# Low parts of weights made by an accumulating DMA in place of VectorE, from the feed-forward block on

## The chip, the cores and the metric

One core of one Trainium2 chip runs the whole program. The metric is the device time of an execution in microseconds.

## What is computed

The reference is a transformer block followed by two retention layers, all in float32, for 512 tokens of width 1024 (528 with 16 meta tokens, padded for the attention). Cut to what matters here:

```
n = rms(h); z = n @ w_in                      # columns: q, k, v, glu, gates
h = h + (sigmoid(g_att)*attention + sigmoid(g_conv)*(conv_branch @ w_conv_out)) @ w_out
up = dwconv3(rms(h) @ w_up)                   # 1024 x 5632
h = h + (silu(gate) * val) @ w_down           # 2816 x 1024
x = rms(h)
for layer in range(2):
    proj = rms(x) @ w_in_2[layer]             # 1024 x 8192
    mix  = [gated short convolution, retention of 8 heads]
    x = x + rms(mix @ w_out_2[layer])         # 2048 x 1024
```

Nearly all of the work is products of activations with weights that are used once.

## The kernel before

TensorE multiplies in a float32r format that drops low bits. Each product is therefore made of three: every operand is split in a high part (the value rounded to float32r) and a low part (the value less the high part), and TensorE adds high x high, high x low and low x high into the same PSUM bank.

The weights come in *units* of 1024 rows by 256 columns (1 MB; smaller for the down projection), in an order fixed by `plan`. A unit is loaded by SyncE's queue into one of three raw tiles `raw0` to `raw2`, as runs of 256 floats; `load(u + 3)` waits for the low part of the last slot of unit u. A unit is cut into two *slots* of 8 blocks of 128x128: by column (`BY_COL`: all 8 row blocks, 128 of the 256 columns, so that a slot reads 8 runs of 512 bytes in each partition of the raw tile) or by k (`BY_K`: 4 row blocks, all 256 columns, 4 KB in one run). Down-projection slots have 3 row blocks, or 2 in the second group. Each slot has a place among three pairs of tiles `whi`, `wlo` (a fourth is used twice at the end of the first retention layer).

`split_hi(s)` is a ScalarE copy raw -> whi, `split_lo(s)` a VectorE subtraction raw - whi -> wlo. `split_hi(s)` waits for the load and for TensorE's last product of the slot that had the place before, `gone[before[s]]`. `take()` gives the next slot to the matmuls and lets `fill` emit the splits of the slots up to two ahead. `products` emits for each block and each part of the columns three matmuls; its first one waits for `t_w`, the token of the slot's low part.

Every engine has its own queue, a `Line`: instructions run in the order in which the Python program emits them, with semaphore waits between. ScalarE and VectorE run the splits and the work on the products' results in that one order. The order of work from the change on: the up projection in two groups of 24 and 20 slots (`tile`: one slot, 48 matmuls of 256 or 258 columns), each followed by the down projection of its part (`two_tiles`: 16 slots each); then for each retention layer four pairs of heads, each with 4 slots for query and key (by k, `two_tiles`), 4 for value and gate (by k) and 8 for the convolution branch (by column, kinds x, c, b, z), among whose matmuls the retention's small products stand as `pieces`; then the output projection in 16 slots (by k). GpSimd's queue `po` holds five instructions at the very start (memsets and an identity matrix) and nothing after.

Of the kernel before, what the change touches and what calls it, by code (L numbers as in the profile page):

```python
# [16 lines left out]
def flat(tokens):  # L17
    for t in tokens:
        if isinstance(t, list):
            yield from flat(t)  # L20
        elif t is not None:
            yield t


class Line:
# [7 lines left out]
        self.ops.append((list(flat(after)), emit, self.count.sem, 1 if mark else 0))  # L33
        return token

    def dma(self, after, dst, src, count):
        token = count.up(16)
        self.ops.append((list(flat(after)), lambda e: e.dma_start(dst, src), count.sem, 16))  # L38
        return token

    def play(self, eng):
# [11 lines left out]
def bass_diff_attention_block_then_retention_layers_kernel(  # L53
# [5 lines left out]
    F = mybir.dt.float32  # L59
    R = mybir.dt.float32r  # L60
    I32 = mybir.dt.int32
    ALU = mybir.AluOpType
    ACT = mybir.ActivationFunctionType
# [17 lines left out]
    with ctx:  # L81
# [103 lines left out]
        def sem(name):  # L185
            return ctx.enter_context(nc.semaphore(name))

        pe, dv, ac, po, sp = Line(sem("pe")), Line(sem("dve")), Line(sem("act")), Line(sem("pool")), Line(sem("sp"))
# [9 lines left out]
        def act(after, o, i, func, **kw):  # L198
            return ac.put(after, lambda e: e.activation(o, i, func, **kw))  # L199

        def tt(after, o, a, b, op):
            return dv.put(after, lambda e: e.tensor_tensor(o, a, b, op))  # L202
# [58 lines left out]
        plan = []  # L261

        def unit(src, slots):
            plan.append((src, slots))

        def cols(w, c0, r0=0, nk=KT, n=256):
            return w[128 * r0:128 * (r0 + nk), c0:c0 + n].rearrange("(k p) c -> p k c", p=128)
# [12 lines left out]
            unit(cols(w_conv_out[0], 256 * j), BY_COL)  # L280
        for j in range(4):
            unit(cols(w_out[0], 256 * j), BY_K)
        GROUPS = [(0, 6), (6, 11)]
        for a, b in GROUPS:
            for j in range(a, b):
# [35 lines left out]
        place = []  # L321
# [6 lines left out]
        def load(u, after):  # L328
            src = plan[u][0]
            n = src.shape[1] * src.shape[2]  # L330
            dst = RAW[u % 3][:, 0:n].rearrange("p (k c) -> p k c", k=src.shape[1])
            t = sp.dma(after, dst, src, raw_count[u % 3])
            loaded.append({k: t for k in range(src.shape[1])})
# [8 lines left out]
            loaded[u][half[0]] = t  # L342

        halves = []

        def split_hi(s):
            u, (k0, k1, c0, c1), _ = slots[s]
            src = plan[u][0]
            n = (k1 - k0) * (c1 - c0)
            raw = RAW[u % 3][:, 0:src.shape[1] * src.shape[2]].rearrange("p (k c) -> p k c", k=src.shape[1])  # L350
            raw = raw[:, k0:k1, c0:c1]
            hi = WHI[place[s]][:, 0:n].rearrange("p (k c) -> p k c", k=k1 - k0)
            lo = WLO[place[s]][:, 0:n].rearrange("p (k c) -> p k c", k=k1 - k0)
            used = extra_free if place[s] == 3 else []
            if before[s] is not None:
                used = [gone[before[s]]]
            halves.append((hi, lo, raw, act([loaded[u][k0], used], hi, raw, ACT.Copy)))

        def split_lo(s):
            u, _, last = slots[s]  # L360
            hi, lo, raw, t_hi = halves[s]
            t_lo = tt([t_hi], lo, raw, hi.bitcast(F), ALU.subtract)
            ready.append((hi, lo, t_lo))
            if last and u + 3 < len(plan):
                load(u + 3, [t_lo])

        def split(s):
            if len(halves) == s:
                split_hi(s)
            split_lo(s)  # L370
# [104 lines left out]
        def whole():  # L475
# [109 lines left out]
            def start():  # L585
# [7 lines left out]
                spread_tokens(0, d, 6)  # L593
                put_x([3], 0, 7, tk[3])
                split_lo(0)
                first_slot[0] = take(0)
                scale_x(0, 0)
# [12 lines left out]
                square_x(4)  # L610
                low_x(3, 0)
                split_lo(1)
                first_slot[1] = take(0)
                first_part(0, 0, 3)
# [774 lines left out]

            for g, (ja, jb) in enumerate(GROUPS):  # L1390
                atok = [None] * 12
# [647 lines left out]
```

How the kernel before makes its waits and increments, by code:

```python
    def play(self, eng):  # L41
        reached = {}
        for after, emit, sem, by in self.ops:
            for count, value in after:
                if reached.get(id(count), 0) < value:
                    eng.wait_ge(count.sem, value)
                    reached[id(count)] = value
            instruction = emit(eng)
            if by:
                instruction.then_inc(sem, by)
# [1933 lines left out]
        @block.sync  # L1984
        def _(eng):
            sp.play(eng)
            for count, value in finished:
                eng.wait_ge(count.sem, value)
```

## Time and profile before

| | us |
|---|---|
| median of 2 runs | 1889.04 (1887.94 to 1890.13) |
| span of the profiled execution, first to last instruction | 1885.5 |
| TensorE busy | 1867.1 (99%) |
| VectorE busy | 1130.1 (60%) |
| ScalarE busy | 737.5 (39%) |
| GpSimd busy | 1.2 |

The profiled execution is known by its span alone; the median of the runs is 3.5 us over it. In the profile PE is TensorE's matmuls and PEld its weight loads, DVE VectorE, ACT ScalarE, POOL GpSimd, SP SyncE; "L191" is a line of the kernel, here that of a helper, so that groups are told apart by their tiles: `wlo<-raw,whi` is an instruction that writes a low tile from a raw and a high tile. "x" is a number of instructions.

### The profile page before, as it was taken

Reading aid. Unit: us, or ns where it says so; the run is one execution under the profiler, and the core shown is the slowest. Engines: PE = TensorE matmul, PEld = TensorE weight load, DVE = VectorE, ACT = ScalarE, POOL = GpSimd, SP = SyncE. Lnnn points to the kernel's source line nnn. Section 1 sums busy time; section 2 is a strip of 40 time slices with the busy share of each in tenths; the row PEclk is TensorE's granted clock in tenths of the full one; section 3 lists DMA queues with packets and bytes.
Section 4 is the critical chain, followed back from the end, with each engine's and each line's share of the span. In section 5 each row is a group of like instructions: output and inputs, shape, how many; then the busy total and the mean of one; then the engine's idle time right before and its main releaser. Section 6 shows DMA issues by size and latency. Waiting matters only on the chain.

```text
span 1885.5 us, 28594 instructions
## 1 busy us (share of the span) xinstructions
PE 1867.1 (99%) x12262; PEld 1688.0 (90%) x12262; DVE 1130.1 (60%) x2035; ACT 737.5 (39%) x1379; POOL 1.2 (0%) x9
## 2 busy tenths in 40 slices
PE   8999999999999999999999999999999999999998
PEld 7999999877899988998898989898899898989887
DVE  5888897577657753666746363636266636454534
ACT  6222333677634432344433333333245333333322
POOL 0000000000000000000000000000000000000000
PEclk9999999999999999999999999999999999999999
DMA  5222222101222223223323233322333232223131
GB/s 185 94 90 90 71 94 87 64 24 46 68 73 92 95 89 107 90 78 94 107 83 102 78 90 90 89 90 80 100 90 90 73 96 78 90 71 108 68 123 45
DMA packets 151837, 163.64 MB, mean 87 GB/s; under 512 B 3495, under 2 KB 148192, under 8 KB 151711
## 3 DMA queue, kind: packets, MB, share of 16 engines
q1 hardware_dynamic: 151694, 161.82, 27.1%
q8 instruction: 96, 1.57, 0.3%
q14 instruction: 31, 0.25, 0.0%
q10 hardware_dynamic: 16, 0.00, 0.0%
HBM read 159.71 MB, written 2.10 MB: 86 GB/s over the span
## 4 chain that ended last, share of the span: by engine, by line
PE 98%; ACT 1%; DVE 1%; DMA 0%; issue 0%; SPq 0%; DVEq 0%
PE ps L191 95%; PE ps L196 2%; ACT nhi L199 0%; DMA xt<-in_x_dram 0%; ACT p L199 0%; DVE ast L973 0%; ACT L199 0%; DVE p L210 0%; DVE wlo L202 0%; ACT whi L199 0%; DVE m L202 0%; ACT ps L199 0%; DVE ga L210 0%; SPq L38 0%; ACT rbc L199 0%
## 5 line engine op out<-in xcount | busy, mean ns | idle before, releaser
L191 PE MATMUL ps<-nhi,whi 128*128 128x256 f32 (+3 forms) x2528 | 682.2, 319 | 3.6 <-DVE nlo L202 2.1
L191 PE MATMUL ps<-nhi,wlo 128*128 128x256 f32 (+3 forms) x2528 | 673.4, 316 | 0.0
L191 PE MATMUL ps<-nlo,whi 128*128 128x256 f32 (+2 forms) x2400 | 637.6, 318 | 0.0
L202 DVE TENSOR_TENSOR wlo<-raw,whi 128x1024 fp32r<-128x1024 f32 (+2 forms) x308 | 365.0, 1189 | 349.7 <-ACT whi L199 349.1
L191 PEld LDWEIGHTS ps<-nhi,whi 128*128 128x128 f32 x2528 | 426.2, 189 | 35.8 <-DVE nlo L202 2.3
L191 PEld LDWEIGHTS ps<-nhi,wlo 128*128 128x128 f32 x2528 | 425.5, 189 | 32.2
L191 PEld LDWEIGHTS ps<-nlo,whi 128*128 128x128 f32 x2400 | 400.8, 189 | 29.1
L199 ACT ACTIVATE whi<-raw 128x1024 fp32r<-128x1024 f32 (+2 forms) x308 | 314.6, 1026 | 261.4 <-PE ps L191 261.0
L210 DVE SCALAR_TENSOR_TENSOR c<-u,cv,c 128x514 f32<-128x514 f32 x240 | 163.2, 748 | 0.0
L191 PE MATMUL ps<-wlo,nhi 128*128 128x256 f32 x512 | 81.6, 281 | 0.0
L191 PE MATMUL ps<-whi,nhi 128*128 128x256 f32 x512 | 81.6, 281 | 0.0
L191 PE MATMUL ps<-whi,nlo 128*128 128x256 f32 x512 | 81.3, 281 | 0.0
L199 ACT ACTIVATE y<-zr,cf 128x512 f32<-128x512 f32 x44 | 35.8, 816 | 113.4 <-DVE zr L202 113.4
L191 PEld LDWEIGHTS ps<-whi,nhi 128*128 128x128 f32 x512 | 70.0, 189 | 0.6
L191 PEld LDWEIGHTS ps<-wlo,nhi 128*128 128x128 f32 x512 | 69.8, 189 | 0.0
L191 PEld LDWEIGHTS ps<-whi,nlo 128*128 128x128 f32 x512 | 69.6, 189 | 0.0
L191 PE MATMUL ps<-alo,whi 128*128 128x512 f32 x176 | 68.5, 389 | 0.0
L191 PE MATMUL ps<-ahi,whi 128*128 128x512 f32 x176 | 68.5, 389 | 0.0
L191 PE MATMUL ps<-ahi,wlo 128*128 128x512 f32 x176 | 68.5, 389 | 0.0
L210 DVE SCALAR_TENSOR_TENSOR y<-zr,cf,y 128x512 f32<-128x512 f32 x88 | 65.9, 748 | 1.8 <-ACT y L199 0.3
L207 DVE TENSOR_SCALAR nx<-ss 128x4 f32<-128x4 f32 (+2 forms) x26 | 4.3, 164 | 102.6 <-ACT ones_d L199 93.9
L199 ACT ACTIVATE ones_d<-ps,osc 128x128 f32<-128x128 f32 x64 | 23.5, 368 | 93.5 <-PE ps L191 91.9
(267 smaller groups left out, 2171.7 us busy)
## 6 DMA issues: line engine op xcount, KB each, us to landing
raw<-in_w_in_dram SPq DMA_DIRECT2D x90, 1024.0 KB, 5.5
raw<-in_w_up_dram SPq DMA_DIRECT2D x22, 1024.0 KB, 5.0
raw<-in_w_out_dram SPq DMA_DIRECT2D x20, 1024.0 KB, 5.1
raw<-in_w_down_dram SPq DMA_DIRECT2D x8, 768.0 KB, 4.9
raw<-in_w_down_dram SPq DMA_DIRECT2D x8, 640.0 KB, 4.6
raw<-in_w_conv_out_dram SPq DMA_DIRECT2D x4, 1024.0 KB, 5.2
xt<-in_x_dram SPq DMA_DIRECT2D x4, 512.0 KB, 5.5
raw<-in_w_in_dram SPq DMA_DIRECT2D x4, 512.0 KB, 8.2
```

The source lines that it names most:

```text
L191: return pe.put(after, lambda e: e.matmul(o, w, m, start=start, stop=stop_), mark)
L196: return pe.put(after, lambda e: e.transpose(o, i, idn), mark)
L199: return ac.put(after, lambda e: e.activation(o, i, func, **kw))
L202: return dv.put(after, lambda e: e.tensor_tensor(o, a, b, op))
L207: return dv.put(after, lambda e: e.tensor_scalar(o, a, s1, s2, op0, op1))
L210: return dv.put(after, lambda e: e.scalar_tensor_tensor(o, a, s, b, op0, op1))
```

## The change

For slots of units from the up projection on (`u >= up_units`), the low part is made in two steps: ScalarE writes the negated high part into the low tile, and then a DMA issued on GpSimd's queue adds the raw weights to it in place. The semaphore of that DMA, one for each of the four places, is what TensorE's first product of the slot and the next load into the raw tile wait for. Slots of earlier units stay as they were. The diff:

```diff
-    def dma(self, after, dst, src, count):
+    def dma(self, after, dst, src, count, **kw):
         token = count.up(16)
-        self.ops.append((list(flat(after)), lambda e: e.dma_start(dst, src), count.sem, 16))
+        self.ops.append((list(flat(after)), lambda e: e.dma_start(dst, src, **kw), count.sem, 16))
         return token
@@
         for j in range(4):
             unit(cols(w_out[0], 256 * j), BY_K)
+        up_units = len(plan)
         GROUPS = [(0, 6), (6, 11)]
@@
         halves = []
+        c_rest = [Count(sem(f"rest{i}")) for i in range(4)]
@@
             hi, lo, raw, t_hi = halves[s]
-            t_lo = tt([t_hi], lo, raw, hi.bitcast(F), ALU.subtract)
+            if u < up_units:
+                t_lo = tt([t_hi], lo, raw, hi.bitcast(F), ALU.subtract)
+            else:
+                t_neg = act([t_hi], lo, hi.bitcast(F), ACT.Copy, scale=-1.0)
+                t_lo = po.dma([t_neg], lo, raw, c_rest[place[s]], accum_op=ALU.add)
             ready.append((hi, lo, t_lo))
             if last and u + 3 < len(plan):
                 load(u + 3, [t_lo])
```

## Rows read from the trace of the kernel before

**Rows 1.** The page: busy time and share of the span; the chain's shares.
```profile
PE 1867.1 (99%) x12262; PEld 1688.0 (90%) x12262; DVE 1130.1 (60%) x2035; ACT 737.5 (39%) x1379; POOL 1.2 (0%) x9
...
PE 98%; ACT 1%; DVE 1%; DMA 0%; issue 0%; SPq 0%; DVEq 0%
```
**Rows 2.** Busy time by stretch: up projection, first layer, all from the change on.
```profile
core 0: us, PE busy (x) PEld busy (x) DVE busy (x) ACT busy (x) POOL busy (x), PEclk, DMA share, GB/s
539.51:679.35 139.84, 139.84 (x1174) 139.66 (x1173) 97.28 (x148) 60.35 (x79) 0.00 (x0) 1.00 0.25 83
913.48:1306.40 392.92, 392.92 (x2234) 341.87 (x2232) 206.58 (x403) 138.90 (x259) 0.00 (x0) 1.00 0.29 86
539.50:1885.50 1346.00, 1339.67 (x8118) 1194.06 (x8116) 724.10 (x1258) 489.82 (x812) 0.00 (x0) 1.00 0.28 88
```
**Rows 3.** Groups of instructions by shape, 539 us to the end: VectorE's and ScalarE's splits.
```profile
L202 DVE TENSOR_TENSOR wlo<-raw,whi 128x1024 fp32r<-128x1024 f32 x202 | 246.0, 1223 | 250.4 <-ACT whi L199 250.1
L202 DVE TENSOR_TENSOR wlo<-raw,whi 128x768 fp32r<-128x768 f32 x24 | 22.9, 958 | 43.3 <-ACT whi L199 43.3
L202 DVE TENSOR_TENSOR wlo<-raw,whi 128x512 fp32r<-128x512 f32 x8 | 5.5, 692 | 7.3 <-ACT whi L199 7.3
...
L199 ACT ACTIVATE whi<-raw 128x1024 fp32r<-128x1024 f32 x202 | 211.8, 1054 | 161.5 <-PE ps L191 161.2
L199 ACT ACTIVATE whi<-raw 128x768 fp32r<-128x768 f32 x24 | 20.1, 841 | 45.2 <-PE ps L191 45.2
L199 ACT ACTIVATE whi<-raw 128x512 fp32r<-128x512 f32 x8 | 5.0, 628 | 9.0 <-PE ps L191 9.0
```
**Rows 4.** Timeline of ScalarE in the up projection: start, duration, instruction, idle before.
```profile
603.39 1.04 ACT L199 ACTIVATE whi<-raw 128x1024 fp32r<-128x1024 f32 x1
...
608.92 1.04 ACT L199 ACTIVATE whi<-raw 128x1024 fp32r<-128x1024 f32 x1
611.86 0.82 ACT L199 ACTIVATE y<-zr,cf 128x512 f32<-128x512 f32 x1 [1.90 <-DVE zr L202]
612.58 1.04 ACT L199 ACTIVATE whi<-raw 128x1024 fp32r<-128x1024 f32 x1
...
618.61 1.05 ACT L199 ACTIVATE whi<-raw 128x1024 fp32r<-128x1024 f32 x1
```
**Rows 5.** Timeline of TensorE at the first products of two slots there.
```profile
610.72 0.40 PE L191 MATMUL ps<-nhi,whi 128*128 128x256 f32 x2
...
627.88 0.40 PE L191 MATMUL ps<-nhi,whi 128*128 128x256 f32 x2
```
**Rows 6.** Timeline of ScalarE in the first and the second down projection.
```profile
712.28 0.84 ACT L199 ACTIVATE whi<-raw 128x768 fp32r<-128x768 f32 x1 [3.29 <-PE ps L191]
...
720.44 0.84 ACT L199 ACTIVATE whi<-raw 128x768 fp32r<-128x768 f32 x1 [3.29 <-PE ps L191]
...
883.76 0.63 ACT L199 ACTIVATE whi<-raw 128x512 fp32r<-128x512 f32 x1 [2.04 <-PE ps L191]
...
890.56 0.63 ACT L199 ACTIVATE whi<-raw 128x512 fp32r<-128x512 f32 x1 [0.83 <-PE ps L191]
```
**Rows 7.** Timeline in the first retention layer: two high parts and their first products.
```profile
1019.90 1.04 ACT L199 ACTIVATE whi<-raw 128x1024 fp32r<-128x1024 f32 x1
...
1025.53 0.39 PE L191 MATMUL ps<-nhi,whi 128*128 128x512 f32 x1
...
1086.72 1.04 ACT L199 ACTIVATE whi<-raw 128x1024 fp32r<-128x1024 f32 x1
...
1092.97 0.48 PE L191 MATMUL ps<-nhi,whi 128*128 128x512 f32 x1
```
**Rows 8.** DMA issues: number, KB each, median us from issue to landing.
```profile
raw<-in_w_in_dram SPq DMA_DIRECT2D x90, 1024.0 KB, 5.5
raw<-in_w_up_dram SPq DMA_DIRECT2D x22, 1024.0 KB, 5.0
...
xt<-in_x_dram SPq DMA_DIRECT2D x4, 512.0 KB, 5.5
raw<-in_w_in_dram SPq DMA_DIRECT2D x4, 512.0 KB, 8.2
out_dram<-outs SPq DMA_DIRECT2D x3, 512.0 KB, 2.6
```
**Rows 9.** The loads' DMA queue: packets, MB, share of 16 engines over the span.
```profile
q1 hardware_dynamic: 151694, 161.82, 27.1%
```

## Prediction

> **What bounds the kernel now.** I read the page's busy shares and its chain first. TensorE is busy 1867.1 of 1885.5 us and owns 98% of the chain; VectorE stands at 60%, ScalarE at 39%, GpSimd at nothing [rows 1]. The table of stretches comes next, for the part that the change touches, 539.5 us to the end: TensorE is busy 1339.67 of 1346.00 us at full granted clock, VectorE 724 us, ScalarE 490 us, GpSimd 0, and the DMA engines 28% [rows 2]. So at most 1346.0 - 1339.7 = 6.3 us can be gained, 0.3%, whatever VectorE is relieved of. A faster result by over 2% (38 us, about what a measurement of this kernel can tell from no change) is out of reach. The question is only whether TensorE starts to wait.
>
> It waits when a slot of weights is not ready. Each slot has 3 buffers in turn; the high part of slot s+3 may be written once slot s is used up, and its products begin two slots later. What must fit between is the budget of the new operation.
>
> **The change, part by part.** From the feed-forward block on there are 236 slots: 204 of 1024 elements a partition, 24 of 768, 8 of 512 (two of the 1024 had their high part before the window, hence 202 in the rows) [rows 3].
>
> Removed: 236 subtractions on VectorE, 246.0 + 22.9 + 5.5 = 274 us with two slots short, and before each the wait for ScalarE behind which all later VectorE work stood [rows 3]. Off the path: worth nothing beyond the 6.3 us.
>
> Added on ScalarE: 236 negating copies. Their nearest row is the high part itself, 1054 ns for 1024 elements and 841 ns for 768 [rows 3]. 204 x 1.05 + 24 x 0.84 + 8 x 0.63 = 240 us, which takes ScalarE from 490 to 730 of 1346 us. ScalarE mostly waits for others behind a high part, so this hides as load; in the chain of one slot it counts in full, in place of the 1.22 us subtraction, and I charge it to the budget below.
>
> Added on GpSimd: 236 accumulating DMAs from SBUF to SBUF, each waiting for its negated copy. Nothing else is queued there, so the wait holds back only the next DMA. TensorE now waits for the landing. The SP queue waits for it too: the load of unit u+3 is behind it, and behind that load only the following loads. A load lands 5.0 us after its issue [rows 8], and the raw tile is wanted some four slots (over 20 us) later, so up to about 15 us of lateness is free there.
>
> **The budgets.** From the start of a high part to its first product, less the high part and the negated copy (2 x 1.04 us for 1024 elements):
> - Feed-forward, up: high parts at 603.39, 608.92, 612.58 and 618.61 us [rows 4]; a slot is 48 matmuls, and counting them from the product at 610.72 [rows 5] a slot lasts 5.72 us, so the four first products are at 610.72, 616.4, 622.2 and 627.88 [rows 5]. Leads 7.3, 7.5, 9.6, 9.3; budgets 5.2, 5.4, 7.5, 7.2, mean 6.3. The pattern repeats over 44 slots. The short ones come from ScalarE's order: the high part stands behind tile work that waits for VectorE.
> - Down: two slots last 8.16 us in the first group (712.28 to 720.44) and 6.80 in the second (883.76 to 890.56) [rows 6]; less two copies of 0.84 that is 6.5 and 5.1 us.
> - Retention layers: ScalarE's order leaves most slots 7 to 11 us, but in every pair of heads three are tight: the second and third of the query/key products (the second counted to 4.2 us in the same way; the third from 1019.90 to 1025.53 [rows 7], 5.6 - 2.1 = 3.5 us), and one among the convolution slots (1086.72 to 1092.97 [rows 7]: 6.25 - 2.08 = 4.2 us); the first convolution slot has 7.4. There are 8 pairs of heads in two layers.
>
> **The unknown, L, from negated copy to landing.** No row has an accumulating DMA, one from SBUF to SBUF, or one from GpSimd. From below: 512 KB stored in 2.6 us [rows 8]. That fits every budget. From above: the slowest 512 KB load took 8.2 us, and a second stream to be read as in a 1 MB load adds up to 5.0 [rows 8]: 13.2 us. Between: slots cut by k are runs of 3 to 4 KB; the 512 KB load with such runs took 5.5 us [rows 8], and the extra read stream and GpSimd's work I put at 0.5 us net, since SBUF is nearer than HBM: L = 6 us, and 5.4 for the smaller down slots. Slots cut by column (44 - 2 in up, 64 in the layers) take 512-byte runs of the raw tile, 1024 of them, and read the copy as well. The 1 MB loads move 1024 packets in 5.0 to 5.5 us [rows 8]; a packet holds an engine 27.1% x 1885.5 x 16 / 151694 = 54 ns [rows 9], so 64 more per engine for the second stream add 3.5 us: L = 9 us. I take 6 and 9, as these rows are the nearest in run and count of packets; 2.6 and 13.2 stay for the range.
>
> **The sum.** Where all slots are short, the loop goes round once in three slots, so an overrun costs a third per slot. Where one is short between long ones, it is paid in full, once.
> - Up: (9 - 6.3) / 3 x 44 = 40 us.
> - Down: nothing in the first group, 0.3 / 3 x 16 = 2 in the second, and 3 for the late high parts at the entries: 5 us.
> - Query/key: 6 - 3.5 = 2.5, one delay for both tight slots, 8 times, less in the first pair of the second layer, which is split otherwise: 18 us.
> - Convolution slots: (9 - 4.2) + (9 - 7.4) = 6.4, 8 times: 51 us.
> - Output projections (32 slots, all by k, budgets mostly 7 to 8.5): 5 us for their entries.
>
> Together 119 us: 1885.5 + 119 = 2004.5. The runs shown have a median 3.5 us over that span, so 2008 us.
>
> The Trainium skill prices the same DMA otherwise. "DMA: Bandwidth & Descriptors", section "Anatomy of one DMA — SWDGE (gpsimd) path", gives a GpSimd-issued DMA about 2.0 us plus its bytes over 436 GB/s. An estimate from that page is 3.2 us for 512 KB, and the sum above would be about nothing. For 1 MB it would say 4.4 us where the loads here took 5.0, from another queue [rows 8]; no run here shows it for an accumulation. The same page, under "Why small descriptors are slow (HBM only)", says that SBUF to SBUF copies don't suffer from short runs.
>
> **Rivals.**
> 1. *Hidden* (the other side: not slower). L stays under about 5 us for both kinds of slot, as the 2.6 us store suggests. It decides at the shortest budgets, 3.5 to 5.2 us. Then only scattered tenths are lost and up to 6.3 gained: 1883 to 1910, middle 1892 us. For it: SBUF on both sides, DMA engines 72% idle. Against: a load of the same size took 5.5. This is what the first rule of the Trainium skill would give.
> 2. *Run length doesn't count*: L = 6 everywhere. Up: the overruns 0.8 and 0.6 in two of four slots, at most 9 us; convolution slots 6 - 4.2 = 1.8, 8 times, 14; the rest as in the sum, 28. 1889 + 51 = 1940 us. It is the case in which the second rule of the Trainium skill holds.
> 3. *Rate, not latency.* If a packet costs 54 ns whatever its size and both streams are fetched as 1024 packets, a slot by column holds each engine 2 x 64 x 54 ns = 6.9 us, and its share of a load 32 x 54 ns = 1.7. 8.6 us exceeds the slot's 5.7: 106 x 2.9 = 307 us, plus 28 elsewhere: 2224 us. It decides where the accumulation takes over 4.0 us of every engine, or GpSimd over 5.7 us to describe 1024 runs. For it: every packet is short; against: the packets measured came from HBM. The same end is reached by a cast from float32 to float32r done element by element.
> 4. *Gain*: the freed VectorE lets ScalarE start high parts earlier and L is short; 6.3 us at most, 1883 us. It can't pass 2%.
>
> **Chances.** Forecast (long runs 6, short 9, give or take 2) 0.37; hidden 0.25; run length without weight 0.13; rate 0.22; gain 0.03. The predicted time is the likeliest case, 2008 us, whose own range is 1955 to 2090 us. The upper bound L = 13.2 (8.2 for long runs) gives 101 + 13 + 38 + 118 + 10 = 280, or 2169 us. The range must take in the hidden case and half of the rate case: 1886 to 2200 us. Slower by over 2% is the forecast, the rate case and most of the second rival, 0.69; within 2% 0.29; faster 0.02.
>
> **What would show it.** Rows of the changed kernel: high part, negated copy and the TensorE row that waits for a DMA into the low tile. Right: landings 6 and 9 us after issue, TensorE's idle time falling on "DMA wlo", about a third of it in the up stage, almost none in the first down group; VectorE down by 274 us and ScalarE up by 240. A wait of ScalarE's tile work behind the copies, or of SP's loads so long that ScalarE waits for raw, would be a step I costed at nothing. The prediction is wrong if the landings are short (TensorE still busy 99%), or if the DMA share nears 1 or GpSimd's issues follow each other without a pause (rate).

## The result and the profile after

The changed kernel takes 2037.72 us (2033.94 to 2041.51, 2 runs) against 1889.04: 1.0787 times the time before, 95% interval 1.0697 to 1.0877. The prediction was 2008 us, in a range of 1886 to 2200. The profiled execution has a span of 2032.0 us, 146.5 more than before; the medians are 148.7 apart. Further down, a time given without an interval is one execution. The two executions of the changed kernel are 7.6 us apart, so a difference of that size between single executions says nothing.

The page after: busy time, the chain's shares by engine and by line, the two DMA queues, and the issues from number and KB to median us to landing. They answer to [rows 1, 8, 9].

```profile
PE 1917.3 (94%) x12262; PEld 1716.6 (84%) x12262; DVE 865.2 (43%) x1799; ACT 977.7 (48%) x1615; POOL 277.8 (14%) x245
...
q0 software_dynamic: 128960, 118.50, 41.0%
q1 hardware_dynamic: 151694, 161.82, 25.9%
...
PE 70%; DMA 14%; ACT 8%; DVE 5%; issue 2%; POOL 0%; SPq 0%; DVEq 0%; ACTq 0%; POOLq 0%
PE ps L191 69%; DMA wlo<-raw 14%; ACT wlo L199 2%; ACT whi L199 2%; PE ps L196 2%; ACT ones_d L199 1%; DVE y L210 1%; DVE sz L210 1%; DVE zr L202 0%; DVE pa L202 0%; ACT xa L199 0%; ACT nhi L199 0%; DVE na L202 0%; ACT sw L199 0%; DVE na L210 0%
...
wlo<-raw POOLq DMA_DIRECT2D x204, 512.0 KB, 6.5
...
raw<-in_w_up_dram SPq DMA_DIRECT2D x22, 1024.0 KB, 6.5
...
wlo<-raw POOLq DMA_DIRECT2D x24, 384.0 KB, 5.0
```

TensorE has the same 12262 matmuls but is idle for 2032.0 - 1917.3 = 114.7 us, 96 more than before, and the chain now holds 14% of DMA and, ahead of it, the two ScalarE copies. It is also *busy* for 50 us more, with the same work. The table of stretches (columns as in [rows 2]) shows the main reason: the granted clock is under full, 0.97 from the change on, where before it was 1.00. Matmul by matmul, 35 of the 50 us lie in stretches at the lower level of the clock, 11 in the matmuls next to a wait, and 4 elsewhere.

```profile
539.51:701.60 162.09, 147.33 (x1190) 145.63 (x1188) 71.11 (x124) 84.65 (x103) 35.01 (x23) 0.97 0.92 154
...
965.90:1389.50 423.60, 402.64 (x2234) 346.63 (x2232) 134.27 (x341) 207.86 (x324) 76.89 (x64) 0.98 0.84 161
539.51:2032.00 1492.49, 1389.35 (x8134) 1223.48 (x8132) 462.17 (x1024) 728.07 (x1046) 274.70 (x234) 0.97 0.82 159
```

The waits of TensorE from the change on (us in total, times, longest) name their cause:

```profile
PE ps L191 <- DMA wlo<-raw: 85.7, 45, 5.3
...
PE ps L191 <- DVE y L210: 6.7, 4, 2.2
...
PE ps L191 <- DVE qr L202: 2.5, 1, 2.5
```

One slot of the up projection in the timeline (ScalarE, GpSimd and TensorE; other rows of the stretch are left out):

```profile
640.55 1.04 ACT L199 ACTIVATE whi<-raw 128x1024 fp32r<-128x1024 f32 x1
641.63 1.06 ACT L199 ACTIVATE wlo<-whi 128x1024 fp32r<-128x1024 f32 x1
...
642.98 1.55 POOL L38 DMA_DIRECT2D wlo<-raw  x1 [6.11 <-ACT wlo L199]
...
651.45 0.77 PE L191 MATMUL ps<-nhi,whi 128*128 128x256 f32 x2 [3.41 <-DMA wlo<-raw]
...
652.87 0.63 PE L191 MATMUL ps<-nhi,whi 128*128 128x256 f32 x2
```

High part and copy take 2.1 us, as priced. The DMA is issued 0.3 us after the copy's end and lands 8.3 us after its issue (a load of 1 MB is under way for most of that time), and TensorE has stood for 3.41 us. Its matmul pairs then take 0.63 to 0.77 us in place of the 0.40 of [rows 5], for a while.

Counting the matmuls of each stage gives the length of the stages in both traces:

| stage | before | after | more | predicted | TensorE's waits, more |
|---|---|---|---|---|---|
| ahead of the change | 539.3 | 541.8 | 2.5 | 0 | -0.4 |
| up projection | 254.2 | 291.8 | 37.6 | 40 | 27.4 |
| down projection | 119.7 | 132.4 | 12.7 | 5 | 7.6 |
| query, key | 181.9 | 209.0 | 27.1 | 18 | 21.9 |
| value, gate | 184.6 | 186.5 | 1.9 | 0 | 3.4 |
| convolution slots | 422.6 | 466.9 | 44.3 | 51 | 22.2 |
| output projections | 180.4 | 200.8 | 20.4 | 5 | 14.3 |
| sum (2.8 us of output follow) | 1882.7 | 2029.2 | 146.5 | 119 | 96.4 |

The last column is the idle time before the stage's own matmuls; it is what the prediction's sum forecast. In the columns ahead of it a stage runs from its first matmul to the next stage's first, so the wait for a stage's first slot stands in the row of the stage before: 7.4 us of waits for other stages' first slots stand in the row of the convolution slots. What the sum of "more" has beyond the sum of waits is slower matmuls.

### The profile page after: what moved, and what is told of

The parts are those of the page before. It is cut to its first block, busy times and chain, and to the rows that moved or that the text cites. A ratio compares the mean times of both kernels' runs of the same rounds, so it can differ in the third digit from the quotient of the medians.

```text
span 2032.0 us, 28897 instructions
## 1 busy us (share of the span) xinstructions
PE 1917.3 (94%) x12262; PEld 1716.6 (84%) x12262; DVE 865.2 (43%) x1799; ACT 977.7 (48%) x1615; POOL 277.8 (14%) x245
## 3 DMA queue, kind: packets, MB, share of 16 engines
q0 software_dynamic: 128960, 118.50, 41.0%
## 4 chain that ended last, share of the span: by engine, by line
PE 70%; DMA 14%; ACT 8%; DVE 5%; issue 2%; POOL 0%; SPq 0%; DVEq 0%; ACTq 0%; POOLq 0%
PE ps L191 69%; DMA wlo<-raw 14%; ACT wlo L199 2%; ACT whi L199 2%; PE ps L196 2%; ACT ones_d L199 1%; DVE y L210 1%; DVE sz L210 1%; DVE zr L202 0%; DVE pa L202 0%; ACT xa L199 0%; ACT nhi L199 0%; DVE na L202 0%; ACT sw L199 0%; DVE na L210 0%
## 5 line engine op out<-in xcount | busy, mean ns | idle before, releaser
L191 PE MATMUL ps<-nhi,whi 128*128 128x256 f32 (+3 forms) x2528 | 694.1, 324 | 75.1 <-DMA wlo<-raw 62.5
L191 PE MATMUL ps<-nhi,wlo 128*128 128x256 f32 (+3 forms) x2528 | 683.2, 320 | 0.0
L191 PE MATMUL ps<-nlo,whi 128*128 128x256 f32 (+2 forms) x2400 | 647.6, 322 | 0.0
L38 POOL DMA_DIRECT2D wlo<-raw x236 | 276.6, 1172 | 1728.1 <-ACT wlo L199 1707.7
L191 PEld LDWEIGHTS ps<-nhi,wlo 128*128 128x128 f32 x2528 | 433.6, 193 | 33.2
L191 PEld LDWEIGHTS ps<-nlo,whi 128*128 128x128 f32 x2400 | 409.0, 193 | 30.1
L199 ACT ACTIVATE wlo<-whi 128x1024 fp32r<-128x1024 f32 (+1 forms) x236 | 241.6, 1024 | 7.4
L202 DVE TENSOR_TENSOR wlo<-raw,whi 128x1024 fp32r<-128x1024 f32 x72 | 88.1, 1224 | 48.0 <-ACT whi L199 47.8
L202 DVE TENSOR_TENSOR zr<-ps,rbc 128x514 f32<-128x514 f32 x44 | 30.4, 694 | 180.0 <-PE ps L191 175.0
L202 DVE TENSOR_TENSOR sd<-ps,far 128x512 f32<-128x512 f32 x16 | 11.0, 687 | 167.3 <-PE ps L191 167.3
```

Of the source, the lines that this page charges most:

```text
L191: return pe.put(after, lambda e: e.matmul(o, w, m, start=start, stop=stop_), mark)
```

## The experiments

Three theories stand against each other. A: TensorE waits for landings that come later than the slot's budget; what makes a landing late (run length, second read stream, loads beside it, GpSimd) is open within it. B: the copies, 240 us of them, disturb ScalarE's order. C: the DMA engines, with a share of 0.82 to 0.92, set the pace.

**The addition on VectorE.** Copies as in the change, no DMA:

```diff
-                t_lo = po.dma([t_neg], lo, raw, c_rest[place[s]], accum_op=ALU.add)
+                t_lo = tt([t_neg], lo, raw, lo.bitcast(F), ALU.add)
```

> The negated copies stay on ScalarE, the addition of the raw weights is done by VectorE in place of the DMA. Theory A (TensorE waits for the landing of the DMA, 6.5 us after its issue, and for nothing else of the change): the loss is gone, 1889 us within 5. Theory B (the 240 us of copies on ScalarE delay the tile work and with it TensorE): most of the loss stays, over 1960 us. Theory C (the DMA engines, busy 80 to 96%, set the pace): 1889 as well, but then with the load's landings back from 6.0-6.5 to 5.0-5.5 us.

Measured: 1908.39 us, 1.0105 times before (1.0088 to 1.0122). So the DMA bears some 129 of the 149 us. B is right in a smaller way: the copies cost 20 us, which the prediction had not priced. Its trace places it:

```profile
PEld ps L191 <- DVE wlo L202: 15.4, 12, 2.6
...
PE ps L191 <- DVE wlo L202: 11.6, 12, 2.1
```

TensorE waits 12 times for a low part that is a copy later than before, mostly where slots follow each other closely: the stages down (7.7 us) and query/key (5.6).

**Slots by k alone, slots by column alone.**

```diff
-            if u < up_units:
+            if u < up_units or slots[s][1][3] - slots[s][1][2] == 128:
```

and in the other kernel `> 128`.

> Only the slots cut by k are made by the DMA, those cut by column by VectorE as before. Theory A: the up projection and the convolution slots lose nothing, the down, query/key and output stages keep their loss (13 + 27 + 20 us in the changed kernel), less where it came from the collision with a neighbour cut by column: 1889 + 50, 1930 to 1950 us. Theory C (rate): with 0.5 MB every second slot only the engines are half free and nearly all loss goes: under 1905.

> The complement: only slots cut by column (half of the up stage and the convolution slots, 106 of 236) by the DMA. Theory A: the up and convolution stages keep their losses (38 + 44 us), the others lose at most what a landing into their first slot costs: 1965 to 1985 us. The losses of this run and of the one with slots by k add up to the whole, 147 us, within 20. Theory C: they add up to less than half of it.

Measured: 1972.58 us with slots by k alone, 1958.09 with slots by column alone. Over the 1888.62 us of the kernel before, measured beside them, that is 84.0 and 69.5 us, together 153.5 against the 149 of the full change: the losses add up, so the bulk is not a shared rate (C), which would vanish when half of the DMAs are gone. But both runs missed their ranges, since the split between the two kinds was wrong: slots by k cost 84, not 50 (1930 to 1950 us were expected), and slots by column 69.5 (1965 to 1985 us were expected). With slots by k alone the down stages lose 19.7 us, query/key 36.1, outputs 23.6, and the convolution slots 0. TensorE's waits for slots by k are not much longer than in the full change, 52.9 against 47.2 us, and in the query/key stages they are no longer, 20.7 against 21.9. What is longer is the time at the lower level of the clock, 27.3 against 13.7 us in the query/key stages. Another part of the miss is in the counting: the expected 50 us were worked out from the rows of the down, query/key and output stages, and waits for their first slots stand in the rows ahead of them.

**One run in place of eight.** For slots by column the DMA reads one run of 4 KB; the kernel leaves out that the right weights are added.

```diff
+                if slots[s][1][3] - slots[s][1][2] == 128:
+                    n = hi.shape[1] * hi.shape[2]
+                    raw, lo_ = RAW[u % 3][:, 0:n], WLO[place[s]][:, 0:n]
...
+                t_lo = po.dma([t_neg], lo_, raw, c_rest[place[s]], accum_op=ALU.add)
```

> Leaves out that the right weights are added: for slots cut by column the DMA reads the first 1024 elements of the raw tile in one run of 4 KB a partition instead of 8 runs of 512 bytes; bytes, waits and counts of DMAs are the same. If run length counts (theory A): landings for them fall from 7.2-8.0 us after issue to the 4.5-5.5 of the slots cut by k, GpSimd's instruction from 1.55 to 0.86 us, and 82 us of loss in the up and convolution stages fall to about 20: 1955 to 1980 us. If it does not count: 2030 to 2040 us.

Measured: 1987.42 us, so 50 of the 149 us go when the runs are long; 1955 to 1980 were expected. The page's queue row and issue row:

```profile
q0 software_dynamic: 33984, 118.50, 32.2%
...
wlo<-raw POOLq DMA_DIRECT2D x204, 512.0 KB, 5.6
```

The same 118.5 MB go in 33984 packets in place of 128960, the median landing comes 0.9 us earlier and GpSimd's instruction takes 0.86 us in place of 1.55:

```profile
603.93 0.86 POOL L38 DMA_DIRECT2D wlo<-raw  x1 [6.49 <-ACT wlo L199]
```

The up and convolution stages lose 34 us in place of 82, where 20 were expected.

**Small loads.** The kernel leaves out seven eighths of each weight load, so most products use old weights.

```diff
+            if u >= up_units + 3:
+                t = sp.dma(after, dst[:, 0:1, :], src[:, 0:1, :], raw_count[u % 3])
...
```

> Leaves out seven eighths of each weight load from the fourth unit of the feed-forward block on (one row block of eight is loaded, so most products use old weights); every wait, split and accumulating DMA is unchanged. Theory A1 (a landing has a floor of 6.4 us for slots cut by column and 4.5 by k after its issue, and 1 to 5 us more come from the load that shares the engines): landings stay at the floor, and the loss falls from 147 to 50-80 us: 1940 to 1970 us. Theory A2 (loads do not matter, late landings have another cause such as GpSimd's queue): landings of 8 to 12 us remain and the time is 2025 to 2040 us. Theory C (the DMA engines' rate sets the pace): without 7/8 of the loads the loss vanishes, under 1900.

Measured: 1986.41 us, 98.5 over the 1887.9 before. Without seven eighths of the loads 51 us less are lost; two thirds remain with the landings alone:

```profile
q0 software_dynamic: 128960, 118.50, 42.4%
q1 hardware_dynamic: 59918, 64.69, 10.1%
...
wlo<-raw POOLq DMA_DIRECT2D x204, 512.0 KB, 6.4
```

From the end of the copy a slot by column lands after 6.7 us at best and a full one by k after 4.8, here as in the full change; there the means over all slots were 7.5 and 8.4 us (up, convolution), 6.8 (query/key), 6.0 (value/gate) and 5.4 (down), with single ones up to 13.0, where here they are 7.0, 7.2, 5.1, 5.1 and 4.4, up to 9.0. The floor costs more than the expected 50 to 80 us, so the run missed its range; C is out as a cause of these two thirds, for it called for under 1900.

**The negation on VectorE.**

```diff
-                t_neg = act([t_hi], lo, hi.bitcast(F), ACT.Copy, scale=-1.0)
+                t_neg = ts([t_hi], lo, hi.bitcast(F), -1.0, ALU.mult)
```

> The negated copy is made by VectorE (tensor_scalar by -1) in place of ScalarE, the DMA is unchanged. Theory A (a chain of high part, copy, DMA against a budget): each chain is shorter by what the copy saves and the 1 us delay of ScalarE's own order is gone, which cost 20 us in the run with the addition on VectorE: 2005 to 2025 us. Against it: VectorE then waits for the high part again, as before the change; if that order is what sets the late high parts, the time stays at 2030 to 2045.

Measured: 2029.71 us, 8 less than the change, no more than the changed kernel's two executions are apart. It is at the edge of the second of the two outcomes: which engine negates matters little beside the landing.

**A plain copy, from two queues.** Both kernels leave out the addition.

```diff
-                t_lo = po.dma([t_neg], lo, raw, c_rest[place[s]], accum_op=ALU.add)
+                t_lo = po.dma([t_neg], lo, raw, c_rest[place[s]])
```

and in the second kernel `sp.dma([t_neg], lo.bitcast(F), raw, c_rest[place[s]])`.

> Leaves out the addition: the same DMA on GpSimd's queue only copies the raw weights over the negated high part. If the second read stream of the accumulation takes engine time (as the prediction charged, 3.5 us for short runs): landings 1.5 to 3 us earlier, the DMA queue's share down from 41% to under 30%, time 1960 to 1990 us. If the accumulation is free: landings, share and 2038 us unchanged within 8 us.

> The same plain copy (addition left out), issued on SyncE's queue, where the loads are, instead of GpSimd's. If GpSimd's making of descriptors is a part of the latency: landings 1 us earlier than in the plain copy on GpSimd's queue, and 10 to 25 us less in time. Against it: SyncE waits for each landing before it issues the next load, so the copies of the next slot queue behind that wait; if this dominates, high parts come to wait for raw and the time is longer than the plain copy's by over 10 us.

Measured: 1931.71 us on GpSimd's queue, faster than the 1960 to 1990 expected, and 1932.18 on SyncE's, neither of the two outcomes expected. The rows of the first and then of the second:

```profile
q0 software_dynamic: 128960, 118.50, 26.8%
...
wlo<-raw POOLq DMA_DIRECT2D x204, 512.0 KB, 3.8
...
wlo<-raw POOLq DMA_DIRECT2D x24, 384.0 KB, 3.7
```

```profile
wlo<-raw SPq DMA_DIRECT2D x204, 512.0 KB, 3.5
...
wlo<-raw SPq DMA_DIRECT2D x24, 384.0 KB, 4.4
```

Adding in place of copying is the largest single price: the same packets take 41.0% of 2032 us against 26.8% of 1930 (103 and 64 ns a packet), the median landing is 2.7 us later, and the time 106 us longer. For a copy, the queue that issues matters little: the landing is 0.3 us later at the median from GpSimd (3.8 against 3.5 us), and the time is the same. No run issues an accumulation from another queue.

The prices of these runs (20, 50, 51 and 106 us) overlap and do not add up to the 149: each says what goes away when one ingredient is taken out of a landing that is late by all of them.

**The low parts last.** The matmuls of a slot in another order, so that the DMA is wanted two thirds of a slot later; the same in the kernel before as a control.

```diff
-            for n, k in enumerate(ks):
-                for c, parts in enumerate(dst):
-                    wh, wl = hi[:, base + n, 128 * c:128 * c + 128], lo[:, base + n, 128 * c:128 * c + 128]
-                    for i, (w, m) in enumerate(((wh, xh), (wh, xl), (wl, xh))):
+            for i, (lw, m) in enumerate(((0, xh), (0, xl), (1, xh))):
+                for n, k in enumerate(ks):
+                    for c, parts in enumerate(dst):
+                        w = (lo if lw else hi)[:, base + n, 128 * c:128 * c + 128]
...
-                            if n == 0 and c == 0 and i == 0 and j == 0:
-                                wait.append(t_w)
+                            if n == 0 and c == 0 and j == 0 and i != 1:
+                                wait.append(t_lo if i else t_hi)
...
```

The loops of the value/gate stages and of the last output projection are changed in the same way.

> The changed kernel with the three products of a slot in another order: all high x high, then all low(activation) x high, then all high x low parts of the weights; the first matmul of a slot waits for the high part alone and the first of its last third for the DMA. Same matmuls, same DMAs. Theory A (landing against budget): every budget grows by two thirds of a slot, 3.8 us (2.7 in the down stages), to 7.3 and more, over most landings (5 to 8 us after the copy); the loss of 147 us falls to 0 to 20: 1889 to 1910 us, the clock back at full and the DMA engines busier than before (over 0.9). Theory C (rate of the DMA engines): the order of products changes nothing, over 2000 us.

> The control: the same order of products in the kernel before, with VectorE's low parts. 1889 us within 5, as TensorE is busy throughout already. If it is slower or faster by more, the order itself has a price or a gain that must be taken out of the run with the DMA.

Measured: 1912.37 us with the DMA, 1.0124 times before (1.0109 to 1.0139), 2 us above the range expected, and 1883.20 us for the control, 0.9974 times before (0.9964 to 0.9984), 5 us faster than before and 1 us outside its range. 125 of the 149 us are gone with every DMA in place, of which the order by itself gives 5, while the landings are no earlier (7.2 us) and the engines busier:

```profile
PE 1871.6 (98%) x12262; PEld 1688.4 (88%) x12262; DVE 865.2 (45%) x1799; ACT 976.8 (51%) x1615; POOL 277.7 (15%) x245
...
q0 software_dynamic: 128960, 118.50, 43.8%
...
wlo<-raw POOLq DMA_DIRECT2D x204, 512.0 KB, 7.2
```

```profile
744.00:860.00 116.00, 114.18 (x958) 113.58 (x957) 49.41 (x73) 65.35 (x77) 29.95 (x20) 1.00 1.07 180
541.00:1900.00 1359.00, 1337.10 (x8066) 1188.73 (x8065) 451.86 (x1001) 722.68 (x1034) 274.62 (x234) 0.99 0.90 173
```

This settles A against C: at a DMA share of 0.90 over the whole rest of the kernel TensorE is busy for 98% of it, and in the second group of the up projection at a share of 1.07 as well. The share is a sum of packet times and can pass 1, so packets of the two queues overlap, and a share near 1 doesn't mean that the engines have no more to give. What remains against the control, 29 us, lies for the most part at the passage between the two retention layers (8.8 us in the first output projection and 8.7 in the query/key stages behind it, with waits of 6.08 and 4.71 us), in the up projection (5.8) and in the last projection (5.3, with a wait of 3.68). The control is a quarter of a per cent faster than the kernel before; it is the best version found, and it has no accumulating DMA.

**Only where the budget is long.**

```diff
+                    if g > 5:
+                        wide.add(len(plan))
...
-            if u < up_units:
+            if u not in wide:
```

`wide` holds the value and gate units of both layers. These are 32 slots; the 64 of the expectation is a miscount, and the price by count would have been 20 us.

> Only the slots of the value and gate products (64 by k, budgets 7 to 9 us, no loss in the changed kernel) by the DMA, the rest by VectorE. Theory A: landings of 5 to 6 us after the copy fit: 1889 us, at most 3 more. If the change costs by itself wherever it stands (copies in ScalarE's queue, DMA traffic): 64/236 of 147, 1925 us or more.

Measured: 1893.74 us, 1.0032 times before (1.0019 to 1.0046), 6 us over the kernel before, where at most 3 were expected, and far under the price by count. In the first layer all three stages have their old length to 0.2 us; the loss is in the first pair of heads of the second layer, 1.5 us in query/key and 4.2 in value/gate, with waits of 1.42 and 2.09 us. That these slots have less lead is the likely reason; it was not tried by itself.

**Pauses by hand.** The kernel before; before every eighth slot TensorE waits for a chain of memsets.

```diff
+        PAUSES = {s: (8, 16, 24, 32, 48)[s // 8 % 5] for s in range(80, 300, 8)}
...
+            if s in PAUSES:
+                hi, lo, t = ready[s]
+                p = gone[-1]
+                for _ in range(PAUSES[s]):
+                    p = po.put([p], lambda e: e.memset(idle, 0.0))
+                ready[s] = (hi, lo, [t, p])
```

> The kernel before, with 28 pauses of TensorE by hand: every eighth slot from the 80th waits for a chain of 8, 16, 24, 32 or 48 small memsets on GpSimd that starts when the slot before is used up. If a pause costs more than its length because the granted clock falls after it (as the changed kernel's trace suggests, 5 of 5 pauses over 3.3 us and some of 1.8 to 2.6): short pauses leave the clock at full, long ones are each followed by a stretch of 3.4 or 6.8 us at half clock, that costs 1.7 to 3.4 us on top. If the clock has nothing to do with them: full clock throughout and the span longer by the sum of the pauses alone.

Measured: 2066.36 us. Two pauses, of 3.53 and of 9.51 us, and the table of stretches around the first and around a pause of 1.71 us (the last of the rows shown):

```profile
641.86 0.50 PE L191 MATMUL ps<-nhi,whi 128*128 128x256 f32 x2 [3.53 <-POOL idle L385]
...
781.01 0.55 PE L191 MATMUL ps<-nhi,whi 128*128 128x256 f32 x1 [9.51 <-POOL idle L385]
```

```profile
630.00:638.00 8.00, 8.00 (x69) 8.00 (x69) 5.40 (x9) 3.98 (x5) 0.00 (x0) 1.00 0.01 3
638.10:641.90 3.80, 0.27 (x3) 0.10 (x2) 3.72 (x6) 1.76 (x2) 2.46 (x16) 1.00 0.51 165
641.90:645.40 3.50, 3.50 (x18) 3.50 (x19) 0.43 (x1) 0.00 (x0) 0.00 (x0) 0.54 0.35 120
645.40:655.00 9.60, 9.60 (x81) 9.60 (x81) 4.45 (x6) 2.29 (x3) 0.00 (x0) 0.99 0.01 3
820.00:840.00 20.00, 18.29 (x154) 18.12 (x153) 12.16 (x17) 8.21 (x11) 1.10 (x8) 1.00 0.20 64
```

After the pause of 3.53 us the granted clock is 0.54, that is mostly the lower of its two levels (1.2 in place of 2.4 GHz), for 3.4 us, with 18 matmuls in 3.5 us where the stretch before has 69 in 8.0; then it is full again. After the pause of 1.71 us it stays at 1.00. Each of the 20 pauses of 3.27 us and more had such a stretch (3.4 to 10.2 us, which can begin while TensorE still stands), of the 8 of at most 2.06 us one had. The span is 178.6 us longer than before, the pauses make 129.2: slower matmuls cost 49 us, 44 of them at the lower level of the clock, 2.5 us for each long pause.

The pauses by hand leave out the lengths from 2.1 to 3.2 us, and the changed kernel has many there. In its trace, from the change on, all 7 waits of 3.3 us and more are followed by a stretch at the lower level, and 12 of the 20 waits of 1.8 to 2.6 us. What parts those 12 from the other 8 was not tried.

## Why the prediction was right, point by point

**What bounds the kernel.** Right: TensorE was covered throughout, the gain was capped at 6.3 us, and VectorE's 265 us less (1130.1 to 865.2) bought nothing.

**ScalarE's copies.** Their load is as priced (977.7 - 737.5 = 240 us). "This hides as load" was not quite true: the run with the addition on VectorE shows 20 us for the copies alone, a term that the sum lacks. There the low part is later by the copy alone, and it came too late 12 times. ScalarE did not come to wait for raw weights behind SyncE's loads; the price of nothing for that step was right.

**The unknown, L.** The two values were 9 us for slots by column and 6 by k. Measured means: 7.5 and 8.4 by column; 6.8, 6.0 and 5.4 by k (query/key, value/gate, down). Both ingredients of the working exist, and each was measured by itself: short runs cost (50 us of time), and the second stream costs (2.7 us of landing, 106 us of time). Their sizes were off: 3.5 us had been charged for the second stream with short runs and 0.5 with long ones, where the best landings after the copy's end are 4.1 us for a copy and 6.7 for an accumulation by column (2.6 more), and 3.2 and 4.8 by k (1.6 more). Left out of the working was the collision with the loads, up to some 4 us for single slots (13.0 at most against 9.0 with small loads); it made 51 us of the time and is the main reason why means lie over the floors of 6.7 and 4.8.

**The budgets and the sum.** What the sum forecast is waiting time, and so it must be held against the last column of the table of stages. The single tight slot among the convolution slots is where it was said to be: in the first layer it waits 2.5 us in each pair of heads, and it lands 6.8 us after the copy, at the floor, against a budget of 4.2. But 9 us was 2.2 too long for this slot, and the first convolution slot, with a budget of 7.4, never waits: the stage's waits are 22.2 us, not 51. With 6.8 in place of 9 the same term gives (6.8 - 4.2) x 8 = 21 us. The up stage waits 27.4 us, not 40; there the loop with the measured mean gives (7.5 - 6.3) / 3 x 44 = 18, so that the rule of a third per slot is too cheap, and the long L hid it. Too small were the terms for stages cut by k: down 5 against 7.6, query/key 18 against 21.9, value/gate 0 against 3.4, outputs 5 against 14.3. For query/key that is L, 1 us too short; the output term was a round 5 us and not worked out.

**What the sum did not have at all** is the slower matmuls. Of the 146.5 us, 96 are idle time and 50 are matmuls that take longer, 35 of those 50 at the lower level of the clock after waits. The waits alone are less than the 119 us forecast, which is 23 us too dear; the absent term is 50 us, and together they put the result 27 us over the forecast.

**What was luck.** That 2008 stands so near 2038, and 44.3 us so near the 51 of the convolution stage, is in good part two misses that offset each other: L by column was too long, and the term for the clock was not there. Right by its working is the cause, TensorE waiting for landings in the slots with the shortest budgets, and the size of the waits to a quarter.

**The rivals.** Hidden: refuted, its point (L under 5 us everywhere) is missed by every slot by column. Run length without weight: refuted by the run with long runs, 50 us. Rate: refuted, by the small loads and, most plainly, by the low parts last. Its condition came true all the same: with slots by column alone a packet takes 25.4% x 1956.0 x 16 / 110240 = 72 ns, so an accumulation takes 64 x 72 ns = 4.6 us of every engine, over the 4.0 at which it was to decide. What failed is its step from there to the time, since the packet times of the two queues overlap.

The estimate from the Trainium skill ("DMA: Bandwidth & Descriptors", "Anatomy of one DMA — SWDGE (gpsimd) path"), 3.2 us for 512 KB, is near the plain copies from GpSimd's queue here (3.8 us after issue at the median, 2.9 at best by k), not the accumulations (6.5 at the median, 4.5 at best for 512 KB by k): the trace agrees for a copy only. The statement of the Trainium skill (the same page, "Why small descriptors are slow (HBM only)") that SBUF to SBUF transfers don't suffer from short runs disagrees with the trace: even plain copies by column land at best 4.1 us after the negated copy's end and those by k 3.2.

## What to carry to other kernels

A transfer put in place of an engine's instruction must be measured against the time between "its input can exist" and "its output is wanted", slot by slot and in the order in which the engines really run, not against the engines' load: here DMA engines that were idle for 72% and a VectorE relieved of 265 us still cost 8%. Where each product has a part that needs the late operand, put that part last: it took back 125 of 149 us and cost nothing. And a wait of TensorE should be priced at more than its length: the waits of 3.3 to 9.5 us made by hand here cost 2.5 us each beyond it, and in the changed kernel 96 us of waits brought 50 us of slower matmuls.

## What the runs showed of the hardware that was not expected

- An accumulating DMA from SBUF to SBUF takes 103 ns a packet where a copy of the same shape takes 64 ns, both a mix of run lengths. Taken apart by size, the packets of 512 bytes take 73 against 50 ns on average, those of 4 KB 340 against 178. With long runs alone the mean over all packets of the queue is 1985.4 x 16 x 32.2% / 33984 = 301 ns.
- A copy issued by GpSimd lands 0.3 us later after its issue than one issued by SyncE, 3.8 and 3.5 us at the median for 512 KB, and the kernels take the same time.
- The DMA share is a sum of packet times and can pass 1: 1.07 over 116 us, with TensorE busy 98% of them.
- GpSimd's DMA instruction takes 1.55 us for 1024 runs and 0.86 us for 128, so it never was near a slot's 5.7 us.
- The granted clock fell to its lower level around each of 20 pauses of 3.27 us and more and once in 8 pauses of up to 2.06 us. It came back after 3.4 to 10.2 us, mostly later behind longer pauses. In the changed kernel 12 of 20 waits of 1.8 to 2.6 us were enough.
- The order of products with the weights' low parts last is a quarter of a per cent faster than the order before (0.9974, 0.9964 to 0.9984). Why was not tried; in the control the part ahead of the up projection is 2.0 us, the up stage 1.7 us and the value/gate stages 1.5 us shorter than before.
